# Decoding attention in a decoder layer: key scores from TensorE to VectorE, and decode steps spread over two projections

## The reference, cut to what matters

```python
x = _half_ffn(x, ffn1_norm, ffn1_in, ffn1_out)
h = _rmsnorm(x, mix_norm)
qa, ka, va, qr, kr, vr, gr, ga, gb = jnp.split(h @ w_in, SPLIT_POINTS, axis=-1)
qa = (_partial_rope(_rmsnorm(qa, a_q_norm), pos) * A_SCALE)        # 3 groups x 8 heads x 64
ka = _partial_rope(_rmsnorm(ka, a_k_norm), pos)
oa, kv_new = attend_a(qa, ka, va)
...
m = (jax.nn.sigmoid(ga) * (oa @ w_pa) + jax.nn.sigmoid(gb) * (ob @ w_pb))
x = x + m @ w_o
x = _half_ffn(x, ffn2_norm, ffn2_in, ffn2_out)
```

```python
g = kv[:, jnp.maximum(cidx, 0)]                  # 128 cached rows, dil apart, and the token's own row
s = jnp.einsum('bthe,btjhe->bthj', q, g[:, :, :, 0])
lse = jax.nn.logsumexp(s, axis=-1)
o = jnp.einsum('bthj,btjhe->bthe', jnp.exp(s - lse[..., None]), g[:, :, :, 1])
```

## Time and profile before

| | |
|---|---|
| Time, three runs | 909.14 us median (908.73 to 910.4) |
| The profiled execution | 910.45 us, its span 908.6 us |
| PE busy | 902.1 us, 99% of the span |
| DVE busy | 600.6 us, 66% |
| ACT busy | 485.1 us, 53% |
| DMA | 281.18 MB, 309 GB/s in the mean |

### The profile page before, as it was taken

The page is one execution under the profiler, slowest core; times in us unless marked ns, Lnnn a source line. Parts: engine busy times, 40 slices in busy tenths (PEclk is TensorE's granted clock), DMA queues, the critical chain, the costliest instruction groups (busy, mean ns, idle before and its releaser), DMA issues.

```text
span 908.6 us, 19528 instructions
## 1 busy us (share of the span) xinstructions
PE 902.1 (99%) x7987; PEld 870.0 (96%) x7987; DVE 600.6 (66%) x870; ACT 485.1 (53%) x746; POOL 216.3 (24%) x233
## 2 busy tenths in 40 slices
PE   9999999999999999999999999999999999999998
PEld 8999999999999999999999999799999999999998
DVE  6666665659975688898788544355558666666543
ACT  6444434445545677677866455246655644443332
POOL 0433330005710000059871113000001043333000
PEclk9999999999999999999999999999999999999999
DMA  9988969999987877889998687849999699997971
GB/s 353 398 317 309 322 228 335 339 363 367 334 308 259 324 255 263 295 312 401 410 337 294 233 268 253 297 166 338 341 366 368 252 346 384 382 366 275 359 216 48
DMA packets 62440, 281.18 MB, mean 309 GB/s; under 512 B 8176, under 2 KB 9328, under 8 KB 60624
## 3 DMA queue, kind: packets, MB, share of 16 engines
q1 hardware_dynamic: 23328, 148.32, 42.8%
q10 hardware_dynamic: 39024, 131.61, 42.6%
HBM read 256.65 MB, written 111.32 MB: 405 GB/s over the span
## 4 chain that ended last, share of the span: by engine, by line
PE 94%; DVE 2%; DMA 1%; issue 1%; ACT 1%; SPq 0%; ACTq 0%; POOL 0%; DVEq 0%
PE acc L446 16%; PE acc L447 16%; PE acc L448 16%; PE att L446 11%; PE att L447 11%; PE att L448 11%; PE aux L1085 2%; PE att L1210 1%; PE att L1144 1%; DMA kv<-cache 1%; PE aux L1049 1%; PE att L827 1%; PE att L1280 1%; PE att L744 1%; PE aux L1308 1%
## 5 line engine op out<-in xcount | busy, mean ns | idle before, releaser
L426 DVE TENSOR_TENSOR wl<-raw,wh 128x1024 fp32r<-128x1024 f32 (+2 forms) x278 | 331.2, 1193 | 220.4 <-ACT wh L420 215.4
L420 ACT ACTIVATE wh<-raw 128x1024 fp32r<-128x1024 f32 (+2 forms) x278 | 275.0, 994 | 186.4 <-PE acc L448 106.2
L446 PE MATMUL acc<-hh,wh 128*128 128x264 f32 x496 | 145.8, 294 | 0.1
L447 PE MATMUL acc<-hl,wh 128*128 128x264 f32 x496 | 140.8, 284 | 0.0
L448 PE MATMUL acc<-hh,wl 128*128 128x264 f32 x496 | 140.6, 284 | 0.0
L446 PE MATMUL acc<-xh,wh 128*128 128x264 f32 x416 | 118.9, 286 | 0.8 <-DVE xl L554 0.8
L446 PE MATMUL att<-xh,wh 128*128 128x264 f32 x416 | 118.6, 285 | 0.3 <-DVE xl L554 0.3
L447 PE MATMUL acc<-xl,wh 128*128 128x264 f32 x416 | 117.9, 283 | 0.0
L448 PE MATMUL att<-xh,wl 128*128 128x264 f32 x416 | 117.8, 283 | 0.0
L448 PE MATMUL acc<-xh,wl 128*128 128x264 f32 x416 | 117.8, 283 | 0.0
L447 PE MATMUL att<-xl,wh 128*128 128x264 f32 x416 | 117.8, 283 | 0.0
(11 more groups left out here) (264 smaller groups left out, 2079.6 us busy)
## 6 DMA issues: line engine op xcount, KB each, us to landing
raw<-w ACTq DMA_DIRECT2D x207, 512.0 KB, 7.1
state<-state_in SPq DMA_DIRECT2D x32, 512.0 KB, 9.5
state_out<-state SPq DMA_DIRECT2D x32, 512.0 KB, 6.1
raw<-w ACTq DMA_DIRECT2D x32, 384.0 KB, 6.0
kv<-cache SPq DMA_DIRECT2D x48, 256.0 KB, 4.7
raw<-w ACTq DMA_DIRECT2D x32, 320.0 KB, 5.3
raw<-w SPq DMA_DIRECT2D x9, 512.0 KB, 8.7
kv_out<-cache SPq DMA_DIRECT2D x3, 960.0 KB, 7.1
```

The costliest lines, as they stand in the source:

```text
L420: nc.scalar.activation(wh[n % HI_RING][:, 0:slot_size(n)], raw[n % RAW_RING][:, 0:slot_size(n)], ACT.Copy).then_inc(hi_done, 1)
L426: nc.vector.tensor_tensor(wl[n % RAW_RING][:, 0:slot_size(n)], raw[n % RAW_RING][:, 0:slot_size(n)], wh[n % HI_RING][:, 0:slot_size(n)].bi ...
L446: nc.tensor.matmul(out, w_hi, xh, start=first, stop=False)
L447: nc.tensor.matmul(out, w_hi, xl, start=False, stop=False)
```

## The change

**Scores on DVE.** The keys are now loaded four sequences at a time, as 6 items of 1 MB in two halves, with the key rows on the partitions and two rows each in the free dimension. POOL packs the queries (`pool_pack`), PE turns them once (`pe_q_rows`, 4 transposes in slot v11 before b0), and per item DVE spreads one query row over its 32 partitions (`dve_key_spread`, a shuffle of 512 columns), multiplies (`dve_key_product`, 2 of 1,024 columns) and sums over the 64 numbers of a head (`dve_key_sum`, 2 of 1,024 columns). The token's own score is 48 matmuls of two columns (`pe_own_score`). The key transposes, their copies, the score matmuls and the clearing are gone.

DVE does its part of a slot (`dec_steps`) ahead of `dve_ahead` in b and g, and behind it in p:

```diff
             for i in range(16):
-                if i == 0:
-                    dve_dec_max(dve)
...
                 att(i)
                 if i % 2:
                     pb_tile(i // 2)
                 dve_ahead(dve, p_pb.q0 + i // 4, i % 4)
+                dec_steps(i)
+                if i in DEC_OUT:
+                    dve_dec_out(dve, DEC_OUT[i])
```

**The prompt's attention** now turns both heads through one bank, and ACT makes both copies. Its first scores write over the banks in which the first query rows were spread, so they wait for the eighth product:

```diff
             else:
                 pe.wait_ge(out_of["act"], p_gb.out0 + KD)
-                pe.wait_ge(dec_act, 4)
+                pe.wait_ge(key_mul, 2 * (G + 1))
```

```diff
-        def turn_bank(r):
-            return bank5 if r else bank6
...
         def pe_turn(pe, i, r):
             pe.wait_ge(att_prob, 2 * i + r + 1)
-            if i:
-                pe.wait_ge(att_copied[r], i)
-            elif r == 0:
-                pe.wait_ge(v_own_done, 1)
+            if i or r:
+                pe.wait_ge(att_copied, 2 * i + r)
...
-        def act_turned(act, i):
+        def act_turned(act, i, r):
...
-        def dve_turned(dve, i):
```

**The input of `p_pa`.** The prompt's columns of `oa` are split as before, the eight decoding columns apart and last, and `p_pa` waits for all of it at its first tile:

```diff
             for t in range(KD):
                 att(16 + t)
+                if 16 + t in DEC_TURN:
+                    act_dec_turn(act, DEC_TURN[16 + t])
                 act_ahead(act, p_ga.q0 + t // 4, t % 4)
+                if t == KD - 1:
+                    act.wait_ge(dec_out, 4)
+                    nc.scalar.activation(oah[:, :, S:T], oa[:, :, S:T], ACT.Copy).then_inc(oa_hi, 1)
...
                     for k in range(4):
-                        if m == 0:
-                            pe.wait_ge(oa_split, k + 1)
+                        if m == 0 and k == 0:
+                            pe.wait_ge(oa_split, 5)
```

```diff
-            for n in range(4):
-                sp_key_load(sp, n)
...
+            for i in range(5):
+                sp_kv_load(sp, "k", i)
+            sp_kv_load(sp, "v", 0)
+            sp_kv_load(sp, "k", 5)
+            sp_kv_load(sp, "v", 1)
             for q in range(p_pb.q0 + 2, fi2.q0):
                 sp.wait_ge(pe_half, 4 * q)
                 roll_more(sp, 2)
+                if q == p_pb.q0 + 2:
+                    sp_kv_load(sp, "v", 2)
+                    sp_kv_load(sp, "v", 3)
```

More of the change, by code:

```diff
@@ new lines, in pool_pad, with pe_q_rows, pe_own_score @@
+        def pool_pad(pool):
+            pool.wait_ge(small_step, 4)
+            nc.gpsimd.memset(dec_pT[:], 0.0).then_inc(q_packed, 1)
+        def pe_q_rows(pe):
+            pe.wait_ge(q_packed, 2 + G)
+            pe.wait_ge(state_new, 2 * STATES)
+            for n in range(4):
+                last = nc.tensor.transpose(bank6[:, n * P:(n + 1) * P], q_pack[:, n], ident)
+            last.then_inc(q_rows, 1)
+        def pe_own_score(pe):
+            pe.wait_ge(os_out, 1)
+            pe.wait_ge(q_packed, 3 + G)
+            for t in range(AT):
+                a = 2 * (AT - 1 - t)
+                for j in range(4):
+                    last = nc.tensor.matmul(bank7[32 * j:32 * j + 32, 0:2], head[:, a:a + 32], own_prod[:, t, j:B:4],
+                                            start=t == 0, stop=t == AT - 1)
+            last.then_inc(own_scored, 1)
@@ new lines, in pe_dec_turn, with act_dec_turn @@
+        def pe_dec_turn(pe, c):
+            pe.wait_ge(dec_dve, 2 * c + 2)
+            if c:
+                pe.wait_ge(dec_out, 2)
+            nc.tensor.transpose(bank7[:, P:2 * P], pR[:, c, 0:P], ident)
+            rsel = TABLES["rsel"][0]
+            nc.tensor.matmul(bank7[0:32 * G, 2 * P:2 * P + 4 * AH], tab[:, rsel + 4 - 4 * c:rsel + 4 - 4 * c + 32 * G],
+                             dec_diag[:], start=True, stop=True).then_inc(dec_pe, 1)
+        def act_dec_turn(act, c):
+            act.wait_ge(dec_pe, c + 1)
+            if c:
+                act.wait_ge(dec_v_done, G)
+            else:
+                act.wait_ge(q_packed, 4 + G)
+            nc.scalar.activation(dec_pT[:, 0:P], bank7[:, P:2 * P], ACT.Copy).then_inc(dec_act, 1)
+            nc.scalar.activation(dec_own[0:32 * G, c], bank7[0:32 * G, 2 * P:2 * P + 4 * AH], ACT.Copy).then_inc(dec_act, 1)
@@ new lines, in pe_dec_v @@
+        def pe_dec_v(pe, i):
+            c, g = i // G, i % G
+            if g == 0:
+                pe.wait_ge(dec_act, 2 * c + 2)
+            pe.wait_ge(kv_in[RING_OF["v", i]], LANDED["v", i])
+            for j in range(4):
+                a = 32 * j + AH * g
+                last = nc.tensor.matmul(bank7[32 * j:32 * j + 32, :], dec_pT[:, a:a + 32], kv_buffer("v", i, j // 2)[:, j % 2],
+                                        start=g == 0, stop=g == G - 1)
+            last.then_inc(dec_v_done, 1)
@@ new lines, in pe_dec_gather @@
+        def pe_dec_gather(pe, c):
+            pe.wait_ge(v_own_done, c + 1)
+            pe.wait_ge(vs_out, AT)
+            for n in range(4):
+                nc.tensor.matmul(bank7[:, 8 * n:8 * n + 8], v_s[:, n * P:(n + 1) * P],
+                                 dec_own[0:32 * G, c, 8 * n:8 * n + 8], start=n == 0, stop=False, skip_group_check=True)
+            for n in range(4):
+                last = nc.tensor.matmul(bank7[:, 8 * n:8 * n + 8], v_own(c)[:, n * P:(n + 1) * P],
+                                        const("own_seq"), start=False, stop=n == 3, skip_group_check=True)
+            last.then_inc(dec_gathered, 1)
@@ L1312, in pe_own_score @@
-        def pe_own_score(pe):
-            for g in range(G):
-                for n in range(4):
-                    last = nc.tensor.matmul(bank7[32 * n:32 * n + 16, G * P + g:G * P + g + 1], own_blk[:, 4 * g + n],
-                                            ones[:, 0:1], start=False, stop=g == G - 1, skip_group_check=True)
-            last.then_inc(dec_pe, 1)
-        NK = G * P + G
-        def dve_dec_max(dve):
-            dve.wait_ge(dec_pe, 1)
-            nc.vector.tensor_reduce(dec_m[:, 0:1], bank7[:, 0:NK], AX.X, ALU.max).then_inc(dec_dve, 1)
-            dve.wait_ge(dec_dve, 1)
-            nc.vector.tensor_scalar(dec_m[:, 1:2], dec_m[:, 0:1], -SCALE, None, ALU.mult).then_inc(dec_dve, 1)
```

444 lines of the change are left out of this document (213 added, 231 removed).

## The result

The changed kernel takes 919.2 us (median of 4 runs, 918.1 to 919.6), the kernel before 909.7 us beside it: ratio 1.010, with a 95% interval of 1.0086 to 1.0116. It is 9.5 us slower, where 908.9 us and a range up to 915.0 had been predicted. The profiled span grew from 908.6 to 917.5 us.

A forecast was written before the change was run, and what follows sets the result against it. PE was taken as the bound, busy 902.1 of 908.6 us. Work leaving PE -15.2, waits +13.3 and clock +1.7 gave -0.2 us, so 908.9 us; 8-in-10 range 902.5 to 915.0, the forecast's own 906.5 to 911.

The forecast's parts named there:

- slower: Chance 0.29 of measuring slower by more than 1.8 us: 0.26 for the slower rivals and a small part of the forecast's.
- the clock: Falls of the granted clock behind p5 and p14, two against one before, at 1.7 us a fall: +1.7 us.
- the five small waits: PE waits: reciprocals in p8, p11; second softmax in g1; value items in p9, p12; together 0 to 5.3 us, 3.0 taken.
- work that leaves PE, net: PE's queue loses 22.1 us (transposes, scores, clearing, turn, gather) and gains 6.9: 15.2 us net.
- DVE's prices: DVE's added work: shuffle 0.68 us, product of 1,024 columns 1.2, sum 1.2; 33 us more in all.
- The 2.0 us of the stepped reduction: Upper bound for a key sum on DVE, from 1,024 columns that step over four tiles; 1.2 us was taken.
- p5, p14, `p_pa`: PE waits for DVE behind the low part: 4.2 us (`dec_diag`, eighth product), 3.4 (masked value rows), 2.7 (last `oal` piece).
- The rival that counted a third fall: Sums as assumed, small waits full, third clock fall behind `p_pa`'s wait: +3.8, 912.9 us; slower in either form 0.26.
- no case of their own: Five 1 MB key items queued at once, bytes unchanged; first wanted some 12 us after issue, so late sums got no case.
- It is wrong if PE's idle time is over 18 us: Sign against the prediction: PE idle under 9 or over 18 us in this stretch.
- The rival "DVE becomes the bound": DVE, key sums 2.0 us: +2.6 at p5, then 0.8 in each of p6–p13; 915.5 us; slower in either form 0.26.
- The whole gain: PE waits nowhere, which would need DVE's results a slot earlier than its queue order allows: 894 to 896 us, chance 0.04.

The follow-up runs named there:

- e13: e4 with the edits of e2 and e3, seventh key product in p2, four rolls (1 MB cache copies) behind the third key item, four in the last phases; 893.8 us.
- e2: Changed kernel with the decode columns of oah (ACT) and last piece of oal (DVE) made ahead of g7's high and low part; 915.9 us.
- e4: Changed kernel with DVE's decoding steps ahead of the low part of the weights in every slot of p; 910.9 us.
- e11: e10 with PE's five long waits filled with extra matmuls, output wrong there; 916.6 us.
- e12: e4 with the eight rolls moved out to the quads before 400 us; 904.1 us.
- e3: Changed kernel with the value matmuls of the second and third items one slot later on PE (p10 and p13); 915.5 us.
- e7: Changed kernel with only the eight rolls issued in b instead of between the value loads; 926.9 us.
- e15: e13 with the decode columns of oah and oal split behind g7's high and low part again; 897.4 us.
- e10: Changed kernel with only the eight rolls moved out to the quads before 400 us; 923.4 us.
- e5: e4 with the eight rolls of p8 to p15 issued in b, four behind the third and four behind the fourth key item; 914.6 us.
- e1: Changed kernel with PE's five long waits filled with extra matmuls, output wrong there; 916.0 us.
- e9: e6 with the eight rolls issued in the quads at about 300 to 400 us; 899.4 us, ratio to before 0.989.
- e6: e5 with the edits of e2 and e3, and the seventh and eighth key products one slot earlier (p2, p3); 908.5 us.
- e8: e7 with PE's five long waits filled with extra matmuls, output wrong there; 922.2 us.

## Why the prediction was wrong

The waits and the low clock behind them were named right as what costs time, and slower had 0.29. What failed is the size of two terms, both too small: the clock, where two falls were counted and four came (1.7 us against 8.5), and the five small waits (3.0 us against 7.7). The gain on PE was 2.3 us larger than said and hid a part of this. Taken from the stretch, with e13's 158.8 us as the same matmuls at full clock and 1.5 us for the fall before (3.4 us at 0.43):

| | predicted | measured |
|---|---|---|
| work that leaves PE, net | -15.2 | 158.8 - (177.8 - 1.5) = -17.5 |
| waits | +13.3 | 19.0 - 1.4 = +17.6 |
| clock | +1.7 | 10.0 - 1.5 = +8.5 |
| sum | -0.2 | +8.6 |

- **PE's work: right, a little low.** The own score took 1.0 us for its 96 records, instead of 2.0: with two columns each they are cheaper than either row that bounded them. The turn of the queries, 0.5 us, lies ahead of the stretch, so -17.0 compares with the -15.2; the last 0.8 us I can't assign. A gather took 1.9 us, as priced.
- **DVE's prices: right.** Shuffle 0.69, product 1.21, sum 1.21 us. The sum's 1.2 was not what 0.55 us for 387 columns scale to in proportion, which is 1.46; it needs a part that does not grow with the columns, by estimate 0.15 us as in the small instruction of the earlier trace rows, and the prediction did not say so. The 2.0 us of the stepped reduction did not come.
- **p5, p14, `p_pa`: right.** 4.3, 3.2 and 2.7 us for 4.2, 3.4 and 2.7. What stands behind the low part reaches PE 2.5 us into the next slot, as the earlier trace rows showed. e2 and e4 confirm the cause.
- **The five small waits: the failing step among the waits.** 3.0 us were taken out of a range of 0 to 5.3. The value items alone took 6.4, g1 0.8 and the probabilities 0.5, together 7.7. The prediction had 5.9 to 8.1 us from the end of the sum to the landing; it was 9.5 in both. The last issue starts 3.2 us behind the first, about as priced, but the slowest part took 6.2 us to land, where the median of the earlier trace rows, 4.7, was the most that was used, and not its upper end of 7.6: an item is there when its last part is. PE was back after 5.9 us at p9, as said. The timeline of PE there:

```profile
589.33 0.28 PE L450 MATMUL acc<-obh,wl 128*128 128x264 f32 x1
593.28 1.06 PE L1387 MATMUL aux<-kv,dec_pT 128*32 128x512 f32 x8 [3.68 <-DMA kv<-cache]
```

- **The clock: the largest miss, 6.8 of the 8.8 us.** Two falls of the earlier trace rows's length were counted. There were four low stretches, at p5, p9, p14 and `p_pa`, and those at p5 and p14 were two and three times as long. The rival that counted a third fall, 912.9 us, went 4.0 of the 10.3 us from the forecast to the measured time. The price of a low microsecond (0.47 taken, 0.43 measured in e11) was right; their number was not. How many low microseconds an execution gets also varies: the mean clocks of the changed kernel's four runs are 0.987, 0.991, 0.989 and 0.987.
- **The loads, given "no case of their own": right for the sums, wrong for the values.** The products waited no more than 0.1 us for key items. In the changed kernel the value items cost little beyond the term above. But they are the reason why mending DVE's order alone gave 8 us and not 15 (e4, e12): those of the second four sequences are awaited while rolls are in flight. The prediction compared the bytes of keys and values with those before and did not look at what else SP issues beside each item.
- **"It is wrong if PE's idle time is over 18 us":** it was 19.0.
- **The rival "DVE becomes the bound": not the cause here, but near.** When the sums were doubled (e14, in e13's order) its first half came, PE waiting 5.0 us more at p5; its second half, a wait in the slots from p6 to p13, did not.
- **"The whole gain would need DVE's results a slot earlier than its queue allows": wrong.** Low parts are made four slots ahead, so the queue did allow it (e4). e13 reaches 893.8, where that rival had 894 to 896 with a chance of 0.04.

## What to carry over

When the work of the bounding engine is cut into a stretch with waits, price each wait as its length and the low clock behind it: in the profiles of this case all 25 waits of PE of 3.0 us or more in the stretch came with a low stretch, which began in the wait or behind it and lasted 3.4 us at the least; so did 10 of the 14 waits from 2.1 to 2.9 us. In the changed kernel it was longest, 10.2 us, at p14, where small matmuls follow. Put what the bounding engine needs next ahead of what is needed four slots later, in every queue: DVE's and ACT's, and keep megabytes that nobody waits for out of the time in which a load is awaited. And read a load of several parts by its slowest part.

## What the runs showed of the hardware

- A wait of 2.7 us at `p_pa`, with PE dense before and behind it, was followed by 3.4 us at 0.50 in the changed kernel, in e3, e7, e12 and e15, by 6.8 us in e4 and e10, and by none in e5. In three of e12's ten runs the mean clock is 1.000, so there it had none either. At p12 a wait of 2.7 us was followed by none in the changed kernel, one of 3.5 us by 3.4 us in e2.
- The clock also falls with no wait: in the kernel before, in e1, e5, e9 and e15 a low stretch of 3.4 us follows the small matmuls of the gather. In the profiles of e4, e6, e8, e11, e12, e13 and e14 none does.
- Filling a wait with matmuls whose result is of no use saved 11.8 us in the profiled stretch (6.8 in the medians) and kept the clock at 1.00 through it.
- A transfer of 128 KB landed in 5.4 us with the rolls moved away (e12), and in 15 to 22 us behind several rolls of 1 MB in the same queue (e4, e5). The weights in ACT's queue, 512 KB each, were slowed beside it: 14.8 us in e4 against 3.9 in e12.
